# 96 places instead of 128 for each expert's tokens in a mixture-of-experts layer

## The reference, cut to what matters

```python
def moe_swiglu(h, router_w, w_gate, w_up, w_down):
    bsz, seq, d = h.shape
    t = h.reshape(bsz * seq, d)
    logits = (t @ router_w).astype(jnp.float32)
    top_v, top_i = lax.top_k(logits, TOP_K)
    ...
    gates = jnp.sum(jax.nn.one_hot(top_i, N_EXPERTS, dtype=jnp.float32) * top_p[..., None], axis=1)
    ...
    for e in range(N_EXPERTS):
        out = out + gates[:, e:e + 1] * swiglu_2(t, w_gate[e], w_up[e], w_down[e])
```

## Time and profile before

| what | value |
|---|---|
| median of 3 runs | 2783.81 us (2783.21 to 2789.51) |
| span of the profiled execution, first to last instruction | 2779.1 us |
| PE busy over the span | 2581.3 us (93%) |
| DVE busy | 1941.8 us (70%) |
| ACT busy | 1431.9 us (52%) |
| moved from HBM over the span | 671.79 MB |

### The profile page before, as it was taken

One profiled execution on the slowest core, in us unless ns is written; L12 is line 12 of the kernel. 1 busy time (PEld: TensorE's weight loads), 2 busy tenths in 40 slices (PEclk: granted clock), 3 DMA queues, 4 the chain that ended last, 5 costly groups with the idle time before them and its releaser, 6 DMA issues. The chain is left out here.

```text
span 2779.1 us, 57909 instructions
## 1 busy us (share of the span) xinstructions
PE 2581.3 (93%) x22787; PEld 1969.1 (71%) x22998; DVE 1941.8 (70%) x2633; ACT 1431.9 (52%) x1753; POOL 14.9 (1%) x12
## 2 busy tenths in 40 slices
PE   6988899999887789998899999899999999999997
PEld 4646677676754467767677767678888888888886
DVE  3366555655535755555565555689999999999997
ACT  3245444443312554444354444377777676777774
POOL 0000000000200000000000000000000000000000
PEclk8979999999978999999899998889999999999999
DMA  7331555554366056544465544449999999999994
GB/s 290 143 161 35 216 199 201 209 201 173 109 229 271 1 201 222 194 162 181 164 251 199 192 168 182 152 178 404 386 395 383 375 392 376 392 381 379 393 376 192
DMA packets 121211, 674.36 MB, mean 243 GB/s; under 512 B 13488, under 2 KB 13968, under 8 KB 67088
## 3 DMA queue, kind: packets, MB, share of 16 engines
q1 hardware_dynamic: 120032, 664.47, 63.4%
q10 hardware_dynamic: 1072, 8.42, 0.8%
HBM read 671.79 MB, written 1.05 MB: 242 GB/s over the span
## 5 line engine op out<-in xcount | busy, mean ns | idle before, releaser
L940 PE MATMUL ps<-projected,normed_or_mix 128*128 128x256 bf16 x1504 | 409.9, 273 | 1.2 <-issue 1.2
L941 PE MATMUL ps<-projected,normed_or_mix 128*128 128x256 bf16 x1504 | 409.9, 273 | 0.0
L1194 PE MATMUL ps<-projected,normed_or_mix 128*128 (+1 forms) x1792 | 304.6, 220 | 3.3 <-DVEq L1342 3.3
L1196 PE MATMUL ps<-projected,normed_or_mix 128*128 (+1 forms) x1792 | 304.7, 220 | 0.0
L1195 PE MATMUL ps<-projected,normed_or_mix 128*128 (+1 forms) x1792 | 304.6, 220 | 0.0
L1196 PE MATMUL ps<-projected,turned 128*128 (+1 forms) x1792 | 303.1, 219 | 0.0
L1195 PE MATMUL ps<-projected,turned 128*128 (+1 forms) x1792 | 303.0, 219 | 0.0
L1194 PE MATMUL ps<-projected,turned 128*128 (+1 forms) x1792 | 303.0, 219 | 0.0
L1315 DVE TENSOR_TENSOR aux<-weights,aux 128x1024 bf16<-128x1024 f32 x224 | 273.0, 1219 | 0.4 <-ACT aux L1270 0.2
L1310 DVE TENSOR_TENSOR normed_or_mix<-weights,normed_or_mix 128x2048 bf16<-128x2048 f32 x111 | 253.9, 2287 | 6.9 <-ACT normed_or_mix L1264 6.9
L1310 DVE TENSOR_TENSOR turned<-weights,turned 128x2048 bf16<-128x2048 f32 x112 | 256.2, 2287 | 3.5 <-ACT turned L1264 3.5
(11 more groups left out here) (385 smaller groups left out, 5863.5 us busy)
## 6 DMA issues: line engine op xcount, KB each, us to landing
weights<-moe SPq DMA_DIRECT2D x224, 1024.0 KB, 7.6
weights<-moe SPq DMA_DIRECT2D x224, 512.0 KB, 5.8
weights<-l_ffn SPq DMA_DIRECT2D x66, 1024.0 KB, 5.1
weights<-ada SPq DMA_DIRECT2D x64, 1024.0 KB, 5.6
weights<-l_ffn SPq DMA_DIRECT2D x66, 512.0 KB, 5.5
weights<-ada SPq DMA_DIRECT2D x64, 512.0 KB, 6.1
weights<-ffn SPq DMA_DIRECT2D x28, 1024.0 KB, 5.1
weights<-w_in SPq DMA_DIRECT2D x24, 948.0 KB, 4.7
```

The source lines that it names most:

```text
L940: pe.matmul(o, hi, h_hi(k), start=(k == 0), stop=False)
L941: pe.matmul(o, hi, h_lo(k), start=False, stop=False)
L1194: pe.matmul(o, hi[:, t], xh, start=(k == 0), stop=False)
L1196: mm = pe.matmul(o, lo[:, t], xh, start=False, stop=(k == KD - 1))
```

## The change

A constant `CAP = 96` takes the place of 128 in the gathered path. The condition for this path becomes a largest count of at most 96. The up products have 96 moving columns in place of 128; the two chunks of a pair lie side by side in PSUM as 2 x 96 columns for gate and 2 x 96 for up; silu and the three gating instructions work on 192 columns in place of 256; the down products have 128x96 weights and write 96 partitions; `keep_output` copies 96 partitions and the scatter sums over 96. Gathering still fills 128 places. No instruction is added, removed or put in another place on any engine: only sizes differ. After the new constant's two lines, what was line n is line n + 2 in the changed kernel.

```diff
+CAP = 96
...
-        def hid(c, w, width=PB, at=0):
-            return PS[:, 6 + c // 2 % 2, w * T + at:w * T + at + width]
+        def hid(c, w, width=CAP, at=0):
+            return PS[:, 6 + c // 2 % 2, w * 2 * CAP + at:w * 2 * CAP + at + width]
...
-                        o, t = hid(j, w, PB, j % 2 * PB), slice(w * D + k * PB, w * D + (k + 1) * PB)
-                        xh, xl = (v[:, bass.ds(e * D + k * PB, PB)] for v in (he_hi, he_lo))
+                        o, t = hid(j, w, CAP, j % 2 * CAP), slice(w * D + k * PB, w * D + (k + 1) * PB)
+                        xh, xl = (v[:, bass.ds(e * D + k * PB, CAP)] for v in (he_hi, he_lo))
...
-                hi, lo = (hid_hl[j // 2 % 2][h][:, j % 2 * PB:(j % 2 + 1) * PB] for h in range(2))
+                hi, lo = (hid_hl[j // 2 % 2][h][:, j % 2 * CAP:(j % 2 + 1) * CAP] for h in range(2))
...
-                    pe.matmul(PS[:, bank, :], hi, w_hi[:, t], start=start, stop=False)
+                    t, o = slice(h * 512, (h + 1) * 512), PS[0:CAP, bank, :]
+                    pe.matmul(o, hi, w_hi[:, t], start=start, stop=False)
...
-                    pe.matmul(PS[:, k // 2, k % 2 * T:(k % 2 + 1) * T], oe[:, k * PB:(k + 1) * PB],
-                              put_t[:, bass.ds(e, 1), :].rearrange("p o t -> p (o t)"), start=False, stop=False,
+                    pe.matmul(PS[:, k // 2, k % 2 * T:(k % 2 + 1) * T], oe[0:CAP, k * PB:(k + 1) * PB],
+                              put_t[0:CAP, bass.ds(e, 1), :].rearrange("p o t -> p (o t)"), start=False, stop=False,
...
-                act.activation(silu[i % 2], hid(2 * i, 0, T), ACT.Silu).then_inc(S.silu_done.sem, 1)
+                act.activation(silu[i % 2][:, 0:2 * CAP], hid(2 * i, 0, 2 * CAP), ACT.Silu).then_inc(S.silu_done.sem, 1)
...
-                f, hi, lo = hid_f[p], hid_hl[p][0], hid_hl[p][1]
+                f, hi, lo, s = (v[:, 0:2 * CAP] for v in (hid_f[p], hid_hl[p][0], hid_hl[p][1], silu[p]))
...
-                dve.tensor_tensor(f, silu[p], hid(2 * i, 1, T), ALU.mult).then_inc(S.prod.sem, 1)
+                dve.tensor_tensor(f, s, hid(2 * i, 1, 2 * CAP), ALU.mult).then_inc(S.prod.sem, 1)
...
-                dve.tensor_copy(oe, PS[:, 4:6, :].rearrange("p a n -> p (a n)")).then_inc(expert_kept.sem, 1)
+                dve.tensor_copy(oe[0:CAP, :], PS[0:CAP, 4:6, :].rearrange("p a n -> p (a n)")).then_inc(expert_kept.sem, 1)
...
-                few = pe.value_load(COUNT[0:1, 0:1], min_val=0, max_val=T) <= PB
+                few = pe.value_load(COUNT[0:1, 0:1], min_val=0, max_val=T) <= CAP
```

More of the change, by code:

```diff
@@ L1201, in down @@
                 pe.wait_ge(S.act_done.sem, m + S.act_done.at(3))
-                hi, lo = (hid_hl[j // 2 % 2][h][:, j % 2 * PB:(j % 2 + 1) * PB] for h in range(2))
+                hi, lo = (hid_hl[j // 2 % 2][h][:, j % 2 * CAP:(j % 2 + 1) * CAP] for h in range(2))
                 w_hi, w_lo = down4[j % SLOTS]
                 for h, bank in enumerate((4, 5)):
-                    t = slice(h * 512, (h + 1) * 512)
-                    pe.matmul(PS[:, bank, :], hi, w_hi[:, t], start=start, stop=False)
-                    pe.matmul(PS[:, bank, :], hi, w_lo[:, t], start=False, stop=False)
-                    mm = pe.matmul(PS[:, bank, :], lo, w_hi[:, t], start=False, stop=stop)
+                    t, o = slice(h * 512, (h + 1) * 512), PS[0:CAP, bank, :]
+                    pe.matmul(o, hi, w_hi[:, t], start=start, stop=False)
+                    pe.matmul(o, hi, w_lo[:, t], start=False, stop=False)
+                    mm = pe.matmul(o, lo, w_hi[:, t], start=False, stop=stop)
                 mm.then_inc(S.down_done.sem, 1)
@@ L2396, in _ @@
             def _(act):
-                few = act.value_load(COUNT[0:1, 0:1], min_val=0, max_val=T) <= PB
+                few = act.value_load(COUNT[0:1, 0:1], min_val=0, max_val=T) <= CAP
                 steps = act_step.n
@@ L2407, in _ @@
             def _(dve):
-                few = dve.value_load(COUNT[0:1, 0:1], min_val=0, max_val=T) <= PB
+                few = dve.value_load(COUNT[0:1, 0:1], min_val=0, max_val=T) <= CAP
                 steps = dve_step.n
```

## The result

| | before | changed |
|---|---|---|
| median of 4 runs each | 2783.51 us (2780.92 to 2789.51) | 2741.03 us (2737.72 to 2742.98) |
| span of the profiled execution | 2779.1 us | 2735.9 us |
| first to 112th gating product | 904.2 us | 862.0 us |

The gain is 42.5 us between the medians, where 28.0 were forecast. 2741.03 us is the lower end of the range, and it is the time of the rival "DVE becomes the limit instead" (2741.8 us, with 862.2 us for the stage).

A forecast was written before the change was run, and what follows sets the result against it. PE was taken to bound the mixture stage, with transfers leading after the change: 110 distances of 7.93 us plus 3.9 give 876.2 us, 28.0 less than 904.2, so 2783.8 - 28.0 = 2755.8 us; range 2741 to 2771 us.

The forecast's parts named there:

- DVE becomes the limit instead: Rival: transfers sustain 418 GB/s, so DVE's 7.73 us a pair leads; stage 862.2 us, total 2741.8 us; chance 0.20.
- What bounds the kernel now: Mixture stage: PE sets the pace at 7.95 us a pair plus 3.5 us scatter an expert; DVE next at 7.90.
- Up products: PE, 96 a pair: from 55.9 to 42.6 ns each with 96 moving columns; any pace below 52 ns would do.
- Down products: PE, 12 a pair: stay at 215.5 ns each, the 96-column weight load hidden under the product; zero change.
- Scatter, silu: Scatter on PE keeps its columns, silu lies under ACT's wait of 2 us a pair; both zero change.
- Gating: DVE's product, cast and low part: together 0.167 us less, 7.73 us a pair plus 1.14 an expert for keep_output.
- What is late next: After the change the weight transfers take the lead over PE (6.68 us) and DVE (7.73 us), at 7.93 us a pair; 0.55.
- Their price for a pair lies between 7.83 us and, from the 387 GB/s at a share of 0.99, 3.146 / 0.391 = 8.05 us: Weight transfers in the mixture stage: bounds on their time for a pair of chunks, with 7.93 us taken in the middle.
- DVE's keep_output then hides in DVE's slack: At an expert's end the copy costs nothing, covered by DVE's slack of 0.2 us a pair, 2.8 us an expert.
- PE did not keep its pace: Rival: weight loads set the 55.9 ns, PE stays at 7.95 us a pair; 2783.8 us, at best about 1 less; 0.12.
- the product over 192 columns shows the gathered path: Rival denied here: an expert over 96 tokens sends all through the general path, 3640 us in all; chance 0.02.
- The clock's case: Rival: PE idles more and its clock falls to 1.2 GHz; slower than before from 68 us at that level; chance 0.03.

The follow-up runs named there:

- E2: Kernel before with only DVE's part of the change: gating on 2 x 96 columns, up products still over 128 columns; 2781.76 us, ratio 0.999.
- E3: Kernel before without the scatter of the first seven experts, whose sums never reach the output; 2754.47 us, ratio 0.9902.
- E1: Only PE's part of the change: 96-column up products and down weights, silu and gating on 256 columns as before; 2759.48 us, ratio 0.9919.
- E4: Changed kernel with 120 places (CAP = 120) in place of 96; 2757.13 us, ratio 0.9911.
- E5: Changed kernel with 64 places and only half of each down weight's low part made, to make DVE cheap; leaves work out; 2714.43 us, ratio 0.9747.
- E7: Changed kernel with keep_output of the first seven experts moved from DVE to ACT; 2728.97 us, ratio 0.9807.
- E6: Changed kernel with 64 places in place of 96, tokens beyond the 64th place left out; 2724.95 us, ratio 0.9787.

## Why the prediction was wrong

*What bounds the kernel now: right.* PE set the pace: E2 takes 0.167 us a pair from DVE and the stage stays at 904.2 us. The scatter was on the path (E3: 3.1 us an expert before DVE takes over), and DVE at 7.90 us was next (E1, E3).

*Up products: right.* 42.4 ns against 42.6. That any pace below 52 ns would do is borne out by E4, where 52.5 ns leave PE with 14 x (96 x 0.0525 + 2.59) + 3.5 = 110.3 us an expert, just under DVE's 14 x 7.86 + 1.12 = 111.2. The 128x128 bf16 loads keep up with products 42.4 ns apart as well as with 55.9.

*Down products: right in effect.* The load of 96 columns lasts longer than that of 128 and stays hidden (below). *Scatter, silu: right.* Neither holds DVE up.

*Gating: right.* DVE was to need 7.73 us for a pair and 1.14 for keep_output. It needs 7.73 and 1.12, with 96 partitions copied in 1.21 us as 128 were in 1.23. The product fell by 68 ns, as said, and the cast by 33, the middle that was taken between its bounds.

*The step that failed is "What is late next"*, "So I expect them to take the lead", and in it the term "Their price for a pair lies between 7.83 us and, from the 387 GB/s at a share of 0.99, 3.146 / 0.391 = 8.05 us". The price is 7.54 us (E5), under DVE's 7.73, and so DVE leads. Both ends of that interval were rates at which the ring had been asked for weights, not rates at which it could give them. The 402 GB/s came from the first expert, where DVE's pace of 7.90 us asks for 3.146 / 7.90 = 398 GB/s. That ACT waited there 0.61 us for a landing was taken as a sign that the transfers held the loop up; the changed kernel and E5 have the same 164 us of such waits, and in the changed kernel DVE never waits behind them, and in E5 it does for 82 us. The 387 GB/s at a share of 0.99 came from PE's pace: 14 pairs, 14 x 3.146 MB, in 114.8 us are 384 GB/s. The step from 0.99 to a capacity of 391 GB/s took the share for a load factor; the share is 0.99 at 386, 1.01 at 403 and 1.02 at 417 GB/s. The 20 us at 418 GB/s, which the prediction held against its own case, are the rate that E5 holds for 750 us.

The Trainium skill says in "Perfetto Trace Analysis", section "Identifying the Most-Contended Engine", that the occupancy of the DMA engines misleads and HBM utilization, which is a rate, is to be used in its place; the shares and rates above agree. Its section "Roofline" puts the practical ceiling of a lone core at some 120% of 358 GB/s, an estimate of 430 GB/s and 7.3 us for a pair, by which DVE would lead as it did. E5 shows 417, 3% less.

A second term fell with it: "DVE's keep_output then hides in DVE's slack". There was no slack, and 7 x 1.12 = 7.8 us that the sum had at nothing were on the path (E7). With both put right, 110 x 7.73 + 7 x 1.12 + 3.22 is 861.4 us, against 862.0 measured. The pair's price alone makes the forecast of the stage 22.0 us too long; the missing keep_output took 7.8 us of that back, so the miss of 14.2 us is smaller than the wrong step.

One reading of the spans is off without harm. The 4.7 us between the profiled span and the median were taken as what lies around the span. On record each run's time is 1.8 us above its own span; the other 2.9 us are the difference between the profiled execution and the median one. The forecast was built on the median and does not use the term.

*The other rivals.* PE did not keep its pace (42.4 ns), the clock stayed at 1.00 in the stage, and the product over 192 columns shows the gathered path. None of them happened. The clock's case does happen at 64 columns, for 2.9 us of the stage (E6).

What stays open: why more of the packets are slow when the rate is lower (below), and what moving a part of DVE's low parts to another engine would bring, which was not tried. By E5 no more than 7.73 - 7.54 = 0.19 us a pair, 21 us in all, is to be had there.

## What to carry to other kernels

In a ring of buffers like this one the rate of the transfers is what the slowest engine lets through, and their busy share near 1.0 does not tell it from their capacity: look instead at whether the last consumer of a slot idles behind them, and at whether the time from issue to landing has grown. Where several engines are within a few per cent of each other, work out each one's time for a whole period, once-a-period work included (scatter, keep_output); a change is then worth the distance to the next of them, and two parts of it, worth 24 and 0 us alone, can be worth 42 together. To learn the price of a resource that is never waited for, make the others cheap in a kernel of its own, as in E5.

## What the runs showed of the hardware

A bf16 weight load of 96 columns lasts longer than one of 128. The loads of the down products in the changed kernel (ns min/median/max), and an up product's beside them:

```profile
L1208 PEld LDWEIGHTS ps<-aux,probs x448: 119/123/123, 1851.3 to 2714.2; 128*96 128x96 bf16 x150
```

```profile
L1196 PEld LDWEIGHTS ps<-projected,turned x1792: 95/98/98, 1846.3 to 2709.0; 128*128 128x128 bf16 x200
```

123 ns against 98; under a product of 215 ns it costs nothing here. In E4 the same loads have 120 columns and a median of 133 ns, in E6 64 columns and 110 ns:

```profile
L1208 PEld LDWEIGHTS ps<-aux,probs x448: 132/133/133, 1853.8 to 2729.9; 128*120 128x120 bf16 x150
L1208 PEld LDWEIGHTS ps<-aux,probs x448: 106/110/177, 1849.5 to 2697.6; 128*64 128x64 bf16 x150
```

So from 64 to 120 columns the time rises by 0.41 ns a column on top of 84 ns, and at 128 it drops. Nor is the 98 ns what a load occupies: in E5 and E6 products with 128x128 weights and 64 moving columns start 29 ns apart. The Trainium skill, in "TensorE: Matmul & The Clock Gate", section "Weight-path perf modes — Fast Weight Load (FWL) and DoubleRow", has a faster load for 128 columns of a type other than float32, and these rows agree: the float32 load of 128 columns lasts 190 ns.

The busy share of the DMA engines stayed at about 1.0 from 386 to 417 GB/s, since at lower rates a larger part of the packets was slow. Counted from the trace over 1900 to 2650 us, packets of 8 KB over 400 ns and of 4 KB over 220 ns took 10.2% of all packet time before, 8.4% in E1, 5.6% in the changed kernel, 4.2% in E7, 2.6% in E6 and 0.3% in E5. The mean packet of 8 KB lasted 322 ns before and 315 in E5, one of 4 KB 180 and 162. This is a correlation over six kernels; its cause was not tested.
